# Moving and stationary operands of the rounded products placed 64 bytes apart, modulo 128

## The chip, the cores and the metric

One NeuronCore of a Trainium2 chip runs the whole program. The metric is device time in microseconds of one execution; the time before is the median of three runs.

## What is computed

The reference is one hybrid layer followed by two mixer layers, on 256 tokens of width 1024, all in float32. Cut to its products:

```python
h = rms_norm(x, norm1_gain)
p = h @ w_in                                  # 1024 x 6176: attention, recurrence, gates
...                                           # attention and a delta-rule recurrence
mixed = gates[..., :D] * y_att + gates[..., D:] * y_rwkv
x = x + mixed @ w_out
x = x + hierarchical_moe(rms_norm(x, norm2_gain), ...)   # 32 experts, top 2
for l in range(2):
    proj = rms_norm_2(x, ...) @ w_in[l]       # 1024 x 3072
    ...                                       # convolutions, two kinds of attention
    x = x + rms_norm_2(mix @ w_out[l], ...)
    f = conv_ffn(rms_norm_2(x, ...), w_up[l], w_conv[l], w_down[l])   # 1024 x 5632, 2816 x 1024
    x = x + rms_norm_2(f, ...)
```

## The kernel before, in words

The large dense products are computed in parts. A float32 operand is split into a rounded high part and the rounded rest, both in the type float32r, and a product is the sum of three: high with high, high with low, low with high. ScalarE writes the high part of a weight piece, VectorE subtracts and writes the low part, and TensorE then runs 8 matmuls (the 8 chunks of 128 of the 1024 inputs) for each part. A matmul has a stationary operand of 128 columns, which a weight load puts in place while the matmul before it runs, and a moving operand of 256 or 512 columns. The experts and most small products stay in float32 and aren't split.

The order is written out by hand for each engine, with semaphores. In the order of time: `front_part` (first projection, 17 pieces of 256 columns, matmuls at L595; three of the pieces, 6 to 8, have x stationary and the weight moving, the others the reverse); the recurrence, with float32 gate tiles in between (L225); `gate_in_parts` (L254), gate pieces 4 to 7, whose pairs of high and low weights lie in three buffers, `first` (pieces 4 and 7), `second` (5) and `third` (6); `mix_part` (L1708 and L1753), first the branch products with `branch_hi/lo`, then the out product with `mixed_hi/lo`, weights in `w_pair`; the experts (L2046 to L2103), whose weights stream into `expert_early`, `expert_ring` and `expert_top`; and `layers_part`, the two last layers, with `w_hi`, `w_lo`, `x_hi`, `x_lo`, `hid_hi` and `hid_lo`: entry products L2842, plain products L2868, value products L2880 with x stationary, and 512-column products L2904 with x or the hidden rows stationary.

SBUF places are given out in two ways. `Room(nc, at)` puts tensors at a fixed byte offset of every partition, one behind the other. `nc.sbuf_tensor` is a stack: it takes the next free place. Two offsets anchor the rooms: `m.room_at`, where the stack stands after the tensors that live long (56640, that is 64 modulo 128), and `m.ring_at`, the start of the experts' ring (81888, that is 96 modulo 128). Inside a tensor, all the slices that the rounded products use start at multiples of 128 bytes from its start, so the start of a tensor gives the place of all its operands modulo 128.

The transfers are issued by SyncE. The expert loads follow one another in ring slots; the first of them are issued between 200 and 270 us, behind waits on the gate, branch and out products.

Of the kernel before, what the change touches and what calls it, by code (L numbers as in the profile page):

```python
# [16 lines left out]
F32 = mybir.dt.float32  # L17
# [3 lines left out]
P = 128  # L21
# [147 lines left out]
KB = 1024  # L169
# [1443 lines left out]
def mix_part(nc, m, a, ctx):  # L1613
# [2 lines left out]
        return ctx.enter_context(nc.semaphore(n))  # L1616

    SPLITS = 2
    room = Room(nc, m.room_at + 8 * KB)
    mixed_hi, mixed_lo = room("mixed_hi", [P, KC, SEQ], F32R), room("mixed_lo", [P, KC, SEQ], F32R)  # L1620
    assert room.at <= m.ring_at
    room = Room(nc, m.ring_at + 64 * KB)
    branch_hi, branch_lo = room("branch_hi", [P, 6, SEQ], F32R), room("branch_lo", [P, 6, SEQ], F32R)
    part = room("gate_part", [P, 2, SEQ])
    room = Room(nc, m.ring_at + 80 * KB)
# [285 lines left out]
EARLY, SLOTS_R = 2, 10  # L1911
# [52 lines left out]
def moe_part(nc, m, a, out, recurrence):  # L1964
# [8 lines left out]
    with ExitStack() as ctx:  # L1973
# [3 lines left out]
        sb = m.room  # L1977
        rec_gpsimd, rec_sync, rec_scalar, rec_tensor, rec_vector = recurrence
        mix_sync, mix_tensor, mix_scalar, mix_vector = mix_part(nc, m, a, ctx)
        logits = sb("logits", [P, TT, NL])  # L1980
        group_max = sb("group_max", [P, TT, 1])
# [180 lines left out]

        assert m.room.at <= m.ring_at - 8 * KB
        layers_gpsimd, layers_sync, layers_tensor, layers_scalar, layers_vector = layers_part(nc, m, a, out, ctx)

        with nc.Block() as block:
# [461 lines left out]
def layers_part(nc, m, a, out, ctx):  # L2628
# [7 lines left out]
    def sb_r(n, s):  # L2636
        return ctx.enter_context(nc.sbuf_tensor(n, s, F32R))
    w_hi = Room(nc, m.room_at)("w_hi", [P, SPLIT, KC * 256], F32R)
    ctx.enter_context(nc.sbuf_tensor("below_layers", [P, (m.ring_at - m.room_at + EARLY * 16 * KB) // 4], F32))
    w_lo = sb_r("w_lo", [P, SPLIT, KC * 256])  # L2640
    x_hi = sb_r("x_hi", [P, KC, SEQ])
    x_lo = sb_r("x_lo", [P, KC, SEQ])
    vec = sb("vec2", [P, P])
# [767 lines left out]
def program(nc, a, out):  # L3411
    with ExitStack() as ctx:
        def sb(n, s):
            return ctx.enter_context(nc.sbuf_tensor(n, s, F32))
        m = Shared()
# [15 lines left out]
        with ExitStack() as one:  # L3431
# [4 lines left out]
            m.att_T = one.enter_context(nc.sbuf_tensor("att_T", [P, 2, SEQ], F32))  # L3436
            m.o_T = one.enter_context(nc.sbuf_tensor("o_T", [P, 4, SEQ], F32))
            m.room_at = nc.sbuf_base
            m.ring_at = (nc.sbuf_usable_end - 9 * 16 * KB) // 32 * 32
            ring = Room(nc, m.ring_at)  # L3440
            m.early = ring("expert_early", [P, EARLY, 2, 2 * D])
            m.first_rows = [one.enter_context(nc.semaphore(f"first_rows{f}")) for f in range(D_EXP // P)]
# [2 lines left out]
            m.landed = [one.enter_context(nc.semaphore(f"landed_{i}")) for i in range(SLOTS_R)]  # L3445
            m.gate_done, m.gate_taken = (one.enter_context(nc.semaphore(n)) for n in ("gate_done", "gate_taken"))
            m.gate_hi, m.gate_lo = (one.enter_context(nc.semaphore(n)) for n in ("gate_hi", "gate_lo"))
            top = Room(nc, m.ring_at + 8 * 16 * KB)
            m.x_hi, m.x_lo = (top(n, [P, KC, SEQ], F32R) for n in ("x1_hi", "x1_lo"))
            first, second, third = (Room(nc, at)(f"gate_pair{i}", [P, 2, KC, 256], F32R)  # L3450
                                    for i, at in enumerate((m.ring_at + 80 * KB, m.ring_at + 64 * KB, m.room_at + 8 * KB)))
            m.gate_pairs = (first, second, third, first)
            with ExitStack() as rec:
                m.w_up = rec.enter_context(nc.sbuf_tensor("w_up", [P, RW], F32))
# [59 lines left out]
```

How the kernel before makes its waits and increments, by code:

```python
def gate_landed(eng, m, g):  # L202
    eng.wait_ge(m.w_landed[gate_slot(g)], 16 * w_loads(gate_slot(g), g + 1, 0))
    return m.w_slots[gate_slot(g)]
# [10 lines left out]
def gate_tiles(pe, m, first, last):  # L216
    for n in range(first, last):
        half, k = divmod(n, KC)
        g, j = divmod(half, 2)
        if n % GATE_TILES == 0:
            gate_landed(pe, m, g)
        if k == 0 and half >= 2:
            pe.wait_ge(m.gate_taken, half - 1)
        mm = pe.matmul(m.ps[:, REC_BANKS + j, 0:SEQ], m.w_slots[gate_slot(g)][:, k, j * P:(j + 1) * P], m.hT[:, k, :],
                       start=(k == 0), stop=(k == KC - 1))
        if k == KC - 1:
            mm.then_inc(m.gate_done, 1)
# [8 lines left out]
def split_gate_low(dve, m, g):  # L237
    pair = m.gate_pairs[g - WHOLE]
    dve.wait_ge(m.gate_hi, g - WHOLE + 1)
    dve.tensor_tensor(pair[:, 1, :, :], m.w_slots[gate_slot(g)][:, :, :], pair[:, 0, :, :].bitcast(F32), ALU.subtract
                      ).then_inc(m.gate_lo, 1)
# [2 lines left out]
def gate_in_parts(pe, m, g, halves=(0, 1)):  # L245
    pair = m.gate_pairs[g - WHOLE]
    for j in halves:
        pe.wait_ge(m.gate_taken, 2 * g + j - 1)
        for part, (w, x) in enumerate(((0, m.x_hi), (0, m.x_lo), (1, m.x_hi))):
            if j == halves[0]:
                pe.wait_ge(m.gate_lo if w else m.gate_hi, g - WHOLE + 1)
# [6 lines left out]
def take_gates(act, m, first, last):  # L259
    for half in range(first, last):
        act.wait_ge(m.gate_done, half + 1)
        g, j = divmod(half, 2)
```

## Time and profile before

| | |
|---|---|
| median of 3 runs | 1359.61 us (1358.38 to 1361.61) |
| span of the profiled execution | 1355.0 us |
| TensorE busy | 1160.0 us, 86% of the span |
| VectorE busy | 737.7 us, 54% |
| ScalarE busy | 487.1 us, 36% |
| bytes read from HBM | 346.93 MB |
| 2868: 2880 matmuls of 256 columns | 134.2 + 134.1 + 132.3 us busy |

Busy times of TensorE are modelled and overlap from one matmul to the next, so a mean duration of 282 ns is not the time that a matmul adds to a run. The time per matmul is read from the starts: in the order of time each line gives the start of a group of alike matmuls and its count, and the difference to the next line's start, divided by the count, is the time of one.

### The profile page before, as it was taken

How to read it: one execution, taken by the hardware profiler on the slowest of the kernel's cores; microseconds unless marked ns; L12 is line 12 of the kernel's file. 1: busy time of each engine (PE TensorE's matmuls, PEld its weight loads, DVE VectorE, ACT ScalarE, POOL GpSimd, SP SyncE). 2: the span in 40 equal slices, each digit the busy share in tenths (PEclk: the TensorE clock that was granted, in tenths of full speed). 3: DMA queues.
4: the chain of work that ended last, by engine and by line, in shares of the span. 5: the costliest groups of instructions: out<-in, count | busy, mean ns of one | idle time of the engine just before them, and what ended most of it. 6: DMA issues, size and time to landing. Idle time of an engine off the chain costs nothing.

```text
span 1355.0 us, 22776 instructions
## 1 busy us (share of the span) xinstructions
PE 1160.0 (86%) x9669; PEld 919.5 (68%) x9669; DVE 737.7 (54%) x1120; ACT 487.1 (36%) x657; POOL 2.6 (0%) x11
## 2 busy tenths in 40 slices
PE   7999989997657366564739999999999999999998
PEld 6998778973213121221314998999998998999997
DVE  5487655852101010010104898877777899877776
ACT  4543435330000000000004546644446556644444
POOL 0000000000000000000000000000000000000000
PEclk9999999998878697788869999999999999999999
DMA  8842225999999999999999646566655436566650
GB/s 270 281 149 63 65 80 210 342 405 416 426 427 424 428 427 424 429 426 427 426 419 361 212 149 179 160 201 186 187 156 179 156 127 181 172 189 187 187 156 31
DMA packets 180986, 349.52 MB, mean 258 GB/s; under 512 B 8140, under 2 KB 154737, under 8 KB 167954
## 3 DMA queue, kind: packets, MB, share of 16 engines
q1 hardware_dynamic: 180394, 347.40, 70.6%
q8 instruction: 79, 1.29, 0.4%
q10 hardware_dynamic: 488, 0.62, 0.2%
q14 instruction: 25, 0.20, 0.0%
HBM read 346.93 MB, written 3.43 MB: 259 GB/s over the span
## 4 chain that ended last, share of the span: by engine, by line
PE 66%; DMA 17%; DVE 3%; issue 2%; SPq 1%; ACT 1%; DVEq 1%; ACTq 0%
PE ps L2868 25%; PE ps L2904 12%; DMA expert_ring<-in_w_expert_up 7%; PE ps L2058 6%; DMA expert_top<-in_w_expert_up 4%; PE ps L2089 4%; DMA expert_early<-in_w_expert_up 2%; DMA expert_ring<-in_w_expert_gate 2%; PE ps L225 2%; PE ps L2046 2%; PE ps L1708 2%; PE ps L2103 2%; PE ps L254 2%; PE ps L2880 2%; PE ps L2842 2%
## 5 line engine op out<-in xcount | busy, mean ns | idle before, releaser
L3216 DVE TENSOR_TENSOR w_lo<-expert_early,w_hi 128x2048 fp32r<-128x2048 f32 x80 | 182.8, 2291 | 25.7 <-ACT w_hi L3010 22.9
L2058 PE MATMUL ps<-expert_ring,w_slot 128*32 128x512 f32 x640 | 113.6, 712 | 96.7 <-DMA expert_ring<-in_w_expert_gate 40.9
L2131 DVE TENSOR_TENSOR hT<-ps,hT 128x512 f32<-128x512 f32 x8 | 8.5, 1068 | 340.9 <-PE ps L2058 340.9
L3010 ACT ACTIVATE w_hi<-expert_early 128x2048 fp32r<-128x2048 f32 x80 | 153.0, 1918 | 56.5 <-PE ps L2904 34.1
L2058 PEld LDWEIGHTS ps<-expert_ring,w_slot 128*32 128x32 f32 x640 | 30.3, 129 | 159.5 <-issue 159.5
L2868 PE MATMUL ps<-x_hi,w_hi 128*128 128x256 f32 x960 | 134.2, 282 | 0.0
L2868 PE MATMUL ps<-x_hi,w_lo 128*128 128x256 f32 x960 | 134.1, 282 | 0.0
L2868 PE MATMUL ps<-x_lo,w_hi 128*128 128x256 f32 x960 | 132.3, 280 | 0.0
L2868 PEld LDWEIGHTS ps<-x_hi,w_hi 128*128 128x128 f32 x960 | 122.9, 188 | 3.8 <-issue 1.6
L2868 PEld LDWEIGHTS ps<-x_hi,w_lo 128*128 128x128 f32 x960 | 123.0, 190 | 0.0
L2868 PEld LDWEIGHTS ps<-x_lo,w_hi 128*128 128x128 f32 x960 | 121.0, 188 | 0.0
L3392 DVE SCALAR_TENSOR_TENSOR ff<-ps,ff_taps,ff 128x254 f32<-128x254 f32 (+1 forms) x176 | 76.8, 478 | 46.5 <-ACT ff L3150 43.3
L3150 ACT ACTIVATE ff<-ps,ff_taps 128x256 f32<-128x256 f32 x88 | 36.9, 471 | 118.2 <-PE ps L2868 117.4
L2058 PE MATMUL ps<-expert_early,w_slot 128*32 128x512 f32 x192 | 51.5, 698 | 23.3 <-DMA expert_ring<-in_w_expert_gate 12.4
L2110 ACT ACTIVATE hT<-ps 128x512 f32<-128x512 f32 x8 | 4.8, 597 | 171.4 <-PE ps L2068 171.4
L2058 PE MATMUL ps<-const,w_slot 128*32 128x512 f32 x48 | 31.8, 827 | 33.1 <-DMA expert_early<-in_w_expert_up 20.5
L2108 ACT ACTIVATE hT<-ps 128x512 f32<-128x512 f32 x8 | 4.8, 597 | 146.4 <-PE ps L2058 146.4
L2089 PE MATMUL ps<-expert_ring,hT 128*32 128x512 f32 x288 | 47.7, 633 | 8.6 <-issue 6.8
L3227 DVE SCALAR_TENSOR_TENSOR att_T<-conf_pad,vec,att_T 128x256 f32<-128x256 f32 x120 | 52.8, 481 | 3.8
L2058 PE MATMUL ps<-expert_top,w_slot 128*32 128x512 f32 x96 | 52.4, 709 | 0.0
L2904 PE MATMUL ps<-w_hi,hid_lo 128*128 128x512 f32 x176 | 48.9, 396 | 0.0
L2904 PE MATMUL ps<-w_lo,hid_hi 128*128 128x512 f32 x176 | 48.8, 395 | 0.0
(531 smaller groups left out, 2095.5 us busy)
## 6 DMA issues: line engine op xcount, KB each, us to landing
expert_ring<-in_w_expert_gate SPq DMA_DIRECT2D x22, 2048.0 KB, 29.4
expert_ring<-in_w_expert_up SPq DMA_DIRECT2D x18, 2048.0 KB, 29.3
expert_early<-in_ffn_up SPq DMA_DIRECT2D x36, 1024.0 KB, 6.0
expert_ring<-in_w_expert_down SPq DMA_DIRECT2D x14, 2048.0 KB, 29.8
w_slot<-in_w_in SPq DMA_DIRECT2D x26, 1024.0 KB, 5.5
expert_early<-in_w_in SPq DMA_DIRECT2D x20, 1024.0 KB, 5.5
expert_early<-in_ffn_down SPq DMA_DIRECT2D x18, 1024.0 KB, 4.9
expert_early<-in_w_expert_gate SPq DMA_DIRECT2D x6, 2048.0 KB, 26.9
```

Of the source, the lines that this page charges most:

```text
L225: mm = pe.matmul(m.ps[:, REC_BANKS + j, 0:SEQ], m.w_slots[gate_slot(g)][:, k, j * P:(j + 1) * P], m.hT[:, k, :], start=(k == 0), stop=(k = ...
L254: mm = pe.matmul(m.ps[:, REC_BANKS + j, 0:SEQ], pair[:, w, k, j * P:(j + 1) * P], x[:, k, :], start=(part == 0 and k == 0), stop=(part == ...
L1708: mm = pe.matmul(out, w[:, pair_of(i), col:col + P], x[y][:, x0 + k, :], start=(p == 0 and k == 0), stop=(p == 2 and k == n - 1))
L2058: mm = pe.matmul(m.ps[rows_of(e), b, :], x_quad[:, k, rows_of(e)], w[e][:, k, :], start=(k == 0), stop=(k == KC - 1))
L2089: mm = pe.matmul(m.ps[rows_of(e), DOWN + j, :], hidden_T[:, f, rows_of(e)], w[e][:, f, j * 512:(j + 1) * 512], start=(f == 0), stop=(f == ...
L2868: mm = pe.matmul(m.ps[:, b, j * SEQ:(j + 1) * SEQ], w[:, s, at(k, j):at(k, j) + P], x[:, k, :], start=(part == 0 and k == 0), stop=(part = ...
L2904: mm = pe.matmul(m.ps[:, banks[2 * t + c], :], xs[:, chunk + k, t * P:(t + 1) * P], w[:, s, k * D + c * 512:k * D + (c + 1) * 512], start= ...
L3010: act.activation(w_hi[:, half_slot(l, i), :], raw_slot(m, i), ACT.Copy).then_inc(S["w_hi"], 1)
L3150: ins = act.activation(ff[:, n % 2, j, :], m.ps[:, b, at:at + SEQ], ACT.Copy, scale=ff_taps[:, 2, j * FF + n:j * FF + n + 1])
L3216: dve.tensor_tensor(w_lo[:, s, :], raw_slot(m, i), w_hi[:, s, :].bitcast(F32), ALU.subtract).then_inc(S["w_lo"], 1)
L3227: dve.scalar_tensor_tensor(conf[:, c, :], src, tap, conf[:, c, :], ALU.mult, ALU.add)
L3392: ins = dve.scalar_tensor_tensor(x, m.ps[:, b, at:at + SEQ - back], ff_taps[:, 2 - back, j * FF + n:j * FF + n + 1], x, ALU.mult, ALU.add)
```

## The change

Only places move. `m.ring_at` is rounded down to a multiple of 128 instead of 32 (81888 becomes 81792). The x operands of the first projection start 64 bytes further on in their room, so do the third gate pair and the branch operands. In the layers, a filler is 64 bytes longer and a small tensor of 64 bytes is put behind `w_lo`, which moves `w_lo` and everything behind it on the stack.

```diff
-    room = Room(nc, m.room_at + 8 * KB)
+    room = Room(nc, m.room_at + 8 * KB + 0)
     mixed_hi, mixed_lo = room("mixed_hi", [P, KC, SEQ], F32R), room("mixed_lo", [P, KC, SEQ], F32R)
     assert room.at <= m.ring_at
-    room = Room(nc, m.ring_at + 64 * KB)
+    room = Room(nc, m.ring_at + 64 * KB + 64)
     branch_hi, branch_lo = room("branch_hi", [P, 6, SEQ], F32R), room("branch_lo", [P, 6, SEQ], F32R)
...
     w_hi = Room(nc, m.room_at)("w_hi", [P, SPLIT, KC * 256], F32R)
-    ctx.enter_context(nc.sbuf_tensor("below_layers", [P, (m.ring_at - m.room_at + EARLY * 16 * KB) // 4], F32))
+    ctx.enter_context(nc.sbuf_tensor("below_layers", [P, (m.ring_at - m.room_at + EARLY * 16 * KB) // 4 + 16], F32))
     w_lo = sb_r("w_lo", [P, SPLIT, KC * 256])
+    sb("beside_w_lo", [P, 16])
     x_hi = sb_r("x_hi", [P, KC, SEQ])
...
-            m.ring_at = (nc.sbuf_usable_end - 9 * 16 * KB) // 32 * 32
+            m.ring_at = (nc.sbuf_usable_end - 9 * 16 * KB) // 128 * 128
...
-            top = Room(nc, m.ring_at + 8 * 16 * KB)
+            top = Room(nc, m.ring_at + 8 * 16 * KB + 64)
             m.x_hi, m.x_lo = (top(n, [P, KC, SEQ], F32R) for n in ("x1_hi", "x1_lo"))
             first, second, third = (Room(nc, at)(f"gate_pair{i}", [P, 2, KC, 256], F32R)
-                                    for i, at in enumerate((m.ring_at + 80 * KB, m.ring_at + 64 * KB, m.room_at + 8 * KB)))
+                                    for i, at in enumerate((m.ring_at + 80 * KB, m.ring_at + 64 * KB, m.room_at + 8 * KB + 64)))
```

The starts of the operands, modulo 128, before and after:

| product | stationary | moving | after |
|---|---|---|---|
| first projection, L595 | w 0 | x 96 | w 0, x 64 |
| first projection, pieces 6 to 8 | x 96 | w 0 | x 64, w 0 |
| gate, pairs first and second, L254 | pair 96 | x 96 | pair 0, x 64 |
| gate, pair third | pair 64 | x 96 | pair 0, x 64 |
| branch, L1708 | w_pair 96 | branch 96 | w_pair 0, branch 64 |
| out, L1708 and L1753 | w_pair 96 | mixed 64 | w_pair 0, mixed 64 |
| layers, L2842 and L2868, high weight part | w_hi 64 | x 96 | w_hi 64, x 0 |
| layers, the same, low weight part | w_lo 96 | x 96 | w_lo 64, x 0 |
| layers, L2880 and L2904, high weight part | x or hidden 96 | w_hi 64 | 0, w_hi 64 |
| layers, the same, low weight part | x or hidden 96 | w_lo 96 | 0, w_lo 64 |

## Rows read from the trace of the kernel before

**Rows 1.** Page, part 2: granted TensorE clock in tenths, 40 slices of 33.9 us.
```profile
PEclk9999999998878697788869999999999999999999
```
**Rows 2.** Windows: stretch, length, busy us (instructions) by engine, clock, DMA share, GB/s.
```profile
22.00:131.00 109.00, 107.40 (x902) 100.26 (x900) 74.31 (x97) 48.07 (x58) 0.00 (x0) 1.00 0.57 179
...
217.00:242.00 25.00, 25.00 (x197) 23.73 (x196) 18.42 (x18) 14.24 (x18) 0.00 (x0) 1.00 0.85 300
...
255.00:288.00 33.00, 32.82 (x276) 32.43 (x275) 22.22 (x27) 10.51 (x11) 0.00 (x0) 1.00 1.04 406
288.00:728.00 440.00, 269.08 (x1923) 107.45 (x1922) 56.93 (x134) 26.64 (x51) 0.00 (x0) 0.81 1.01 422
...
1163.00:1346.00 183.00, 183.00 (x1307) 171.76 (x1307) 137.95 (x194) 91.77 (x109) 0.00 (x0) 1.00 0.54 159
```
**Rows 3.** Waits of PE, first in 22 to 131 us, then in 740 to 1355 us.
```profile
PE ps L595 <- DVE w_lo L782: 0.2, 1, 0.2
...
PE ps L2842 <- DVE w_lo L3216: 0.5, 1, 0.5
```
**Rows 4.** Order of time, PE: start us, us; branch product, first and twenty-ninth matmul.
```profile
242.16 0.40 PE L1708 MATMUL ps<-branch_hi,w_pair 128*128 128x256 f32 x2
...
245.52 0.64 PE L1708 MATMUL ps<-branch_hi,w_pair 128*128 128x256 f32 x4
```
**Rows 5.** Order of time, PE: gate product, third pair, then first pair.
```profile
234.53 1.10 PE L254 MATMUL ps<-x_lo,gate_pair 128*128 128x256 f32 x8
235.47 2.06 PE L254 MATMUL ps<-x_hi,gate_pair 128*128 128x256 f32 x16
...
238.32 2.08 PE L254 MATMUL ps<-x_hi,gate_pair 128*128 128x256 f32 x16
240.24 1.12 PE L254 MATMUL ps<-x_lo,gate_pair 128*128 128x256 f32 x8
```
**Rows 6.** Order of time, PE: plain product of the layers, its three parts.
```profile
902.84 1.10 PE L2868 MATMUL ps<-x_hi,w_hi 128*128 128x256 f32 x8
...
904.72 1.12 PE L2868 MATMUL ps<-x_hi,w_lo 128*128 128x256 f32 x8
905.68 1.10 PE L2868 MATMUL ps<-x_hi,w_hi 128*128 128x256 f32 x8
```
**Rows 7.** Order of time, PE: first projection, weight stationary, then x stationary.
```profile
44.48 1.12 PE L595 MATMUL ps<-x_hi,w_hi 128*128 128x256 f32 x8
...
46.40 1.11 PE L595 MATMUL ps<-x_hi,w_lo 128*128 128x256 f32 x8
...
64.13 1.10 PE L595 MATMUL ps<-w_hi,x_hi 128*128 128x256 f32 x8
...
66.94 0.28 PE L595 MATMUL ps<-w_hi,x_hi 128*128 128x256 f32 x1
```
**Rows 8.** Chain of work that ended last: start us, us, what, count.
```profile
266.45 11.52 PE ps L1708 x96
...
484.67 3.57 PE ps L2046 x32
...
860.66 17.00 PE ps L2868 x144
```
**Rows 9.** Order of time, PE: 512-column product, 12 matmuls, then the next line's start.
```profile
914.14 1.09 PE L2904 MATMUL ps<-w_hi,hid_hi 128*128 128x512 f32 x4
...
916.93 0.75 PE L2868 MATMUL ps<-x_hi,w_hi 128*128 128x256 f32 x5
```
**Rows 10.** Groups by line and shape: busy us, mean ns | idle before; the split's low part.
```profile
L3216 DVE TENSOR_TENSOR w_lo<-expert_early,w_hi 128x2048 fp32r<-128x2048 f32 x80 | 182.8, 2291 | 25.7 <-ACT w_hi L3010 22.9 <-issue 1.1
...
L3216 DVE TENSOR_TENSOR w_lo<-w_slot,w_hi 128x2048 fp32r<-128x2048 f32 x18 | 41.3, 2293 | 7.4 <-ACT w_hi L3010 6.0 <-issue 0.9
```
**Rows 11.** DMA issues: count, KB each, median us from issue to landing.
```profile
expert_early<-in_ffn_up SPq DMA_DIRECT2D x36, 1024.0 KB, 6.0
...
w_slot<-in_ffn_up SPq DMA_DIRECT2D x8, 1024.0 KB, 6.1
```

## Prediction

> **What bounds the kernel now.** I read the granted clock first, then the busy time by stage, then who waits for whom, then the order of time inside the stages that TensorE bounds. The clock line [rows 1] stands at 9 tenths or more in the stages where the change acts; it dips only in the middle. The stage table [rows 2] splits the span in three. From 22 to 131 us (first projection) and from 217 to 242 us (gate product) TensorE is busy for nearly the whole stretch; from about 255 to 728 us the DMA engines are full (share 1.01 to 1.04, 406 to 422 GB/s) and TensorE has room; from 728 us to the end TensorE is busy all the time, in 1163 to 1346 us for 183.00 of 183.00 us. The waits [rows 3] agree: in the first projection the rounded operands hold TensorE up for 0.2 us, in the two last layers for 0.5 us. So the product runs as fast as TensorE takes its matmuls, and the quantity to look at is the time from the start of one matmul to the start of the next, called the spacing here. "Busy" in the profile overlaps and can't give it; starts in the order of time do.
>
> **The spacing by placement.** The rounded products differ in one thing that this change touches: where the stationary operand starts, modulo 128 bytes, against the moving one. "Below" and "above" say where the stationary one lies.
> - 0 apart. Branch product: 28 matmuls from 242.16 to 245.52 us, 120.0 ns each [rows 4]. Gate product, first and second pair: 16 in 238.32 to 240.24, 120.0 ns [rows 5]. Layers with the low weight part: 8 in 904.72 to 905.68, 120.0 ns [rows 6].
> - 32 apart, stationary below. Layers with the high weight part: 16 in 902.84 to 904.72, 117.5 ns [rows 6]. Gate product, third pair: 8 in 234.53 to 235.47, 117.5 ns [rows 5]; the same line of code, the same x operand, another pair buffer. First projection with x stationary: 24 in 64.13 to 66.94, 117.1 ns [rows 7].
> - 32 apart, stationary above. First projection with the weight stationary: 16 in 44.48 to 46.40, 120.0 ns [rows 7]; the out product: 96 in 11.52 us, 120.0 ns [rows 8].
> A whole run of 144 in the layers takes 17.00 us [rows 8], 118.1 ns; two parts at 117.5 and one at 120.0 would make 118.3, so the two levels carry the stage. The placement therefore shifts the spacing by 2.6 ns, and 117.4 (between 117.5 and 117.1) against 120.0 are the prices I use.
> The 512-column products run at 2.79 us for 12, 232.5 ns [rows 9]; they mix placements 0 and 32 apart, and I see no difference between their three parts.
> The Trainium skill, "TensorE: Matmul & The Clock Gate", Part 2, says that loading the next weights doesn't take read bandwidth from the running matmul, because the two operands have a read port each. By that rule no placement matters and the sum would be zero. Rows 5 disagree by 2.5 ns a matmul, so I don't take zero as my forecast, but it stays a rival.
>
> **What the change does, part by part.** No instruction, wait or transfer is added or removed. The three placements become one: 64 apart everywhere. Counts of 256-column matmuls on the path:
> - now at 120.0: first projection with the weight stationary 576, gate product 144, branch product 144, low weight part in the layers 960 + 64 + 64 (plain, entry and value products), value products with the high part 128. Together 2080, of which 864 lie before 250 us and 1216 in the layers.
> - now at 117.4: first projection with x stationary 144, third gate pair 48, high weight part in the layers 1920 + 128. Together 2240.
> - left out: the first piece of the first projection, 48 matmuls whose spacing waits for x.
> - not on the path: the out product, 192 matmuls at 266 to 288 us. The DMA engines are full there [rows 2], and what follows ends with a transfer. Its price is nothing; were the transfers not full there, it would be worth 192 x 2.6 ns = 0.5 us.
> With a spacing g after the change, the difference is 2080 x (g - 120.0) + 2240 x (g - 117.4) ns.
> The trace doesn't show 64 apart in a rounded product. Bounds: below, the nearest row with a weight load and a matmul that both last about as long as here is the gather product, 32 in 3.57 us, 111.6 ns [rows 8]: -17.5 - 13.0 = -30.5 us. Above, the worst placement seen, 120.0: +5.8 us. I take g = 117.4, the better of the two levels: three placements give 120.0 (0), 120.0 (32 above) and 117.4 (32 below), and a smooth wave through these three over 128 bytes gives 117.4 at 64 as well. That is 2080 x -2.6 ns = -5.4 us: -3.2 us in the layers and -2.2 us ahead of them.
> The -2.2 us pass through the stage that the transfers bound only if these start earlier. They do: the expert loads around 200 to 250 us are issued behind waits on the gate and branch products, whose inputs come from TensorE's order, and the full stretch then keeps its length.
> For the 512-column products (720) both placements seen cost the same, so I take 0; -1.8 us (230 ns, twice the 115 of the next part) and +1 us are the ends.
> What is late next: in 1163 to 1346 us VectorE is busy for 137.95 and ScalarE for 91.77 of 183.00 us [rows 2], so a matmul that is 2% faster finds its operands ready.
> Side effects. The whole ring moves from 96 to 0 modulo 128. The split on VectorE costs 2291 ns from a ring buffer (at 96) and 2293 from a weight slot (at 64) [rows 10]: the same. The loads of 1 MB land in 6.0 us in the ring and in 6.1 in the slot [rows 11]: the same. Both at nothing; if the full stretch of 440 us moved by 0.3% either way, 1.3 us.
>
> **Rivals.**
> 1. Placement at 64 removes more of the contention. The shape of the three points is thin evidence for a wave; the curve could dip at 64. With g = 115, about as far below 117.4 as this is below 120: -10.4 - 5.4 = -15.8, and -1.8 for the 512-column products, -17.6 us. Chance 0.18.
> 2. All of it goes: 111.6 and twice that for 512 columns (223.2): -30.5 - 6.7 = -37 us. Against it: the 512-column matmuls pay for a longer time than one weight load lasts, and all three placements pay at least 5.8 ns over 111.6, while placement moves 2.6. Chance 0.05. The same page of the Trainium skill, section "Back-to-back issue gap", gives N / 2.4 + 2.5, 109.2 ns for 256 columns; by it, used as an estimate, the sum would be about -41 us on these matmuls. No row of a rounded product comes near.
> 3. Slower: the contention repeats every 64 bytes, not every 128, so 64 apart is 0 apart again. Then g = 120.0: nothing is gained where it costs 120.0, and the high weight part of the layers, the largest group, loses 2240 x 2.6 ns = +5.8 us, with up to +1 for the rest. It decides from g = 118.7 on. For it: 0 apart is the worst placement, and nothing in the trace separates a period of 64 from one of 128 except that 32 above and 32 below differ. That difference speaks against a strict period of 64, not against a second dip and peak. Chance 0.20.
> 4. No change that can be measured, g between 118.0 and 119.3, or no effect of placement as such, or a buffer that doesn't end up where the text of the change says. Gains at 120.0 and losses at 117.4 cancel. Chance 0.17.
> My forecast has 0.40.
>
> **How the numbers follow.** The span is 1355.0 us, the median of the runs 1359.6; the 4.6 us around the span don't change. Forecast 1359.6 - 5.4 = 1354.2. The range reaches from rival 1 (1342) to rival 3 (1359.6 + 6.8 = 1366.4): I take 1343 to 1366, which leaves out rival 2 and the tails of 1 and 3. What a measurement of this kernel can tell from no change is about 0.2%, 2.7 us. Faster by more than that: 0.40 + 0.18 + 0.05 = 0.63, less 0.02 for the weak end of the forecast, 0.61. Within: 0.17 + 0.02 = 0.19. Slower: 0.20.
>
> **What would show it.** Right: in the order of time, 8 matmuls of any rounded 256-column product take 0.94 us from start to start, whichever part; a run of 144 in the layers takes 16.9 us, not 17.00; the first full transfer stretch begins 2 us earlier and is as long as before; the end comes 3 us earlier than that beyond. Wrong: 0.96 everywhere (rival 3), 0.92 or less (rival 1), 0.89 (rival 2). If the spacing falls and the end doesn't move, the step "TensorE bounds these stages" fails. If the full stretch changes its length, it is the transfers into the moved ring.

## The result and the profile after

The change takes 1346.82 us (1346.28 to 1348.65, 5 runs) against 1358.81 us for the kernel before in the same measurement: ratio 0.9917, 95% interval 0.9906 to 0.9927, 12.0 us less. A second measurement of the same kernel gave 1347.23 against 1358.21 us, ratio 0.9919 (0.9906 to 0.9933). The forecast was 5.4 us less. Work and counts are the same as before: 22776 instructions, 349.52 MB in the page's line on packets.

The clock stands at 9 tenths where it stood there before [rows 1], and the waits in the layers are of the same kind and size [rows 3]. What moved is seen in the order of time. In the chain of work that ended last (start us, us, what, count), the second layer part of the kernel after the change:

```profile
848.23 2.05 PE ps L2811 x16
850.28 5.52 PE ps L2843 x48
855.80 16.32 PE ps L2869 x144
872.12 5.57 PE ps L2905 x24
877.69 11.31 PE ps L2869 x96
889.00 5.57 PE ps L2905 x24
```

L2869 is L2868 of before, L2905 is L2904, and L2843, the entry product, is L2842. The 144 matmuls took 17.00 us before [rows 8] and take 16.32 now: 113.3 ns each, where the forecast had 117.4. The 96 behind them take 11.31 us: 117.8 ns each. So there is not one spacing for 64 apart but two, called the quick and the slow level below. The order of time of TensorE (start us, us, instruction, count) shows that each is steady over all three parts of the product. First the quick kind, then the slow one:

```profile
860.17 1.07 PE L2869 MATMUL ps<-x_hi,w_lo 128*128 128x256 f32 x8
861.08 1.07 PE L2869 MATMUL ps<-x_hi,w_hi 128*128 128x256 f32 x8
861.98 1.07 PE L2869 MATMUL ps<-x_lo,w_hi 128*128 128x256 f32 x8
862.89 1.07 PE L2869 MATMUL ps<-x_hi,w_lo 128*128 128x256 f32 x8
...
901.95 1.10 PE L2869 MATMUL ps<-x_hi,w_lo 128*128 128x256 f32 x8
902.89 1.11 PE L2869 MATMUL ps<-x_hi,w_hi 128*128 128x256 f32 x8
903.83 1.10 PE L2869 MATMUL ps<-x_lo,w_hi 128*128 128x256 f32 x8
904.78 1.10 PE L2869 MATMUL ps<-x_hi,w_lo 128*128 128x256 f32 x8
```

Starts 0.90 or 0.91 us apart for 8 matmuls are 113 ns; 0.94 or 0.95 are 118 ns. In [rows 6] the high weight part took 117.5 and the low part 120.0; the difference between the parts has gone, as it should when both weights lie 64 from x.

By stage, from the starts of the products: the layers' first rounded matmul starts at 737.17 instead of 739.77 us, 2.6 us earlier, and the span ends at 1346.0 instead of 1355.0. So 2.6 us were won ahead of the layers and 6.4 us in them (608.8 instead of 615.3 us). The 6.4 repeats in a second profile; the 2.6 belongs to this pair of executions. After the change the first rounded matmul of the first projection starts at 15.25 us, 1.8 us later than before (13.47). From there to the first expert matmul it takes 282.9 instead of 286.3 us, 3.4 less. The expert matmuls then stretch over 429.0 instead of 429.9 us, and over 429.1 to 431.8 in the other profiles of the block. The mean spacing over all plain, entry and value products of the layers, worked out from all starts in the trace with those over 150 ns left out, fell from 118.19 to 116.42 ns, and that of the 512-column products from 232.8 to 231.4. In the first projection the mean fell from 119.3 to 116.7, in gate and branch from 119.3 and 120.0 to 117.8.

### The profile page after: what moved, and what is told of

Same layout as the page of the kernel before. It is cut to its first block, busy times and chain, and to the rows that moved or that the text cites. A ratio compares the mean times of both kernels' runs of the same rounds, so it can differ in the third digit from the quotient of the medians.

```text
span 1346.0 us, 22776 instructions
## 1 busy us (share of the span) xinstructions
PE 1152.3 (86%) x9669; PEld 911.4 (68%) x9669; DVE 737.3 (55%) x1120; ACT 487.2 (36%) x657; POOL 2.6 (0%) x11
## 2 busy tenths in 40 slices
DMA packets 180986, 349.52 MB, mean 260 GB/s; under 512 B 8140, under 2 KB 154737, under 8 KB 167954
## 4 chain that ended last, share of the span: by engine, by line
PE 65%; DMA 17%; DVE 3%; issue 2%; SPq 1%; ACT 1%; DVEq 1%; ACTq 0%
PE ps L2869 25%; PE ps L2905 11%; DMA expert_ring<-in_w_expert_up 7%; PE ps L2058 6%; DMA expert_top<-in_w_expert_up 4%; PE ps L2089 4%; DMA expert_early<-in_w_expert_up 2%; DMA expert_ring<-in_w_expert_gate 2%; PE ps L225 2%; PE ps L2046 2%; PE ps L2103 2%; PE ps L254 2%; PE ps L1708 2%; PE ps L2881 2%; PE ps L2843 2%
## 5 line engine op out<-in xcount | busy, mean ns | idle before, releaser
L2058 PE MATMUL ps<-expert_ring,w_slot 128*32 128x512 f32 x640 | 116.3, 721 | 95.6 <-DMA expert_ring<-in_w_expert_gate 42.1
L3217 DVE TENSOR_TENSOR w_lo<-expert_early,w_hi 128x2048 fp32r<-128x2048 f32 x80 | 182.8, 2291 | 24.3 <-ACT w_hi L3011 21.5
L2869 PE MATMUL ps<-x_hi,w_hi 128*128 128x256 f32 x960 | 133.5, 282 | 0.0
L2869 PE MATMUL ps<-x_hi,w_lo 128*128 128x256 f32 x960 | 131.3, 278 | 0.0
L2869 PE MATMUL ps<-x_lo,w_hi 128*128 128x256 f32 x960 | 131.2, 279 | 0.0
L2869 PEld LDWEIGHTS ps<-x_hi,w_hi 128*128 128x128 f32 x960 | 122.1, 189 | 3.8 <-issue 1.6
L2869 PEld LDWEIGHTS ps<-x_lo,w_hi 128*128 128x128 f32 x960 | 120.6, 189 | 0.0
L2869 PEld LDWEIGHTS ps<-x_hi,w_lo 128*128 128x128 f32 x960 | 120.2, 187 | 0.0
L2905 PE MATMUL ps<-w_hi,hid_lo 128*128 128x512 f32 x176 | 48.8, 395 | 0.0
L2905 PE MATMUL ps<-w_hi,hid_hi 128*128 128x512 f32 x176 | 48.5, 393 | 0.0
```

The costliest lines, as they stand in the source:

```text
L2058: mm = pe.matmul(m.ps[rows_of(e), b, :], x_quad[:, k, rows_of(e)], w[e][:, k, :], start=(k == 0), stop=(k == KC - 1))
L2869: mm = pe.matmul(m.ps[:, b, j * SEQ:(j + 1) * SEQ], w[:, s, at(k, j):at(k, j) + P], x[:, k, :], start=(part == 0 and k == 0), stop=(part = ...
L2905: mm = pe.matmul(m.ps[:, banks[2 * t + c], :], xs[:, chunk + k, t * P:(t + 1) * P], w[:, s, k * D + c * 512:k * D + (c + 1) * 512], start= ...
L3217: dve.tensor_tensor(w_lo[:, s, :], raw_slot(m, i), w_hi[:, s, :].bitcast(F32), ALU.subtract).then_inc(S["w_lo"], 1)
```

## The experiments

The mean of a stage below is worked out as above; "quick" is the share of its 256-column spacings under 115 ns, which is the level of 113.3.

**The layers alone, and all the rest alone.** Both are the changed kernel with one side taken back.

```diff
--- the layers alone
-    ... EARLY * 16 * KB) // 4 + 16], F32))
+    ... EARLY * 16 * KB) // 4 + 24], F32))
...
-            m.ring_at = (nc.sbuf_usable_end - 9 * 16 * KB) // 128 * 128
+            m.ring_at = (nc.sbuf_usable_end - 9 * 16 * KB) // 32 * 32
...
-            top = Room(nc, m.ring_at + 8 * 16 * KB + 64)
+            top = Room(nc, m.ring_at + 8 * 16 * KB)
--- all the rest alone
-    ... EARLY * 16 * KB) // 4 + 16], F32))
+    ... EARLY * 16 * KB) // 4 + 24], F32))
-    sb("beside_w_lo", [P, 16])
```

(In the first, the third gate pair and the branch operands go back as well.)

> Only the operands of the two last layers are placed 64 bytes apart; the ring, the first projection, the gate and the branch products lie as in the kernel before. Theory (spacing of the rounded matmuls, stage by stage, adds up): the layers gained 6.4 us of span in the profile of the change, so 1358.8 - 6.4 = about 1352.4 us, ratio 0.995; the first transfer-bound stretch begins and ends as before (728 us). Rival (the gain is from the ring's new place and the transfers into it): no gain, 1358 to 1360.

Measured: 1354.95 against 1357.87 us, ratio 0.9974 (0.9964 to 0.9985), 2.9 us less.

> The reverse: everything ahead of the layers as in the change, the ring at 0 modulo 128 included, the layers' operands as before (w_hi 32 below x, w_lo at x). Theory: the end of the transfer-bound stretch comes 2.6 us earlier and the layers take as long as before: about 1356.2 us, ratio 0.998; with e1 it adds up to the whole. Rival (ring and transfers): nearly the whole gain of 12 us stands here.

Measured: 1353.37 us, ratio 0.9964 (0.9952 to 0.9976), 4.5 us less. Both sides gain, so the ring and its transfers aren't the cause of the whole. But the sum, 7.4 us, falls short of the 12.0, and the halves are the wrong way round. The traces say why in part. With the layers alone, the layers took 610.6 us (741.47 to 1352.1), 4.6 less than before, not 6.4; their quick share was 0.11, not the change's 0.32, although every operand lay at the same place modulo 128. With the rest alone, the layers took 615.2 us, as before, and the part ahead of them 4.7 us less than before; there the gate product ran with a quick share of 0.42 and the branch product with 0.99, at 113.4 ns, where the change's first profile had 117.8 for both. The same placement, then, gives different levels, and in the layers this is 1.8 of the 4.6 us that the sum lacks. The other 2.8 are about what three ratios with intervals of some 1.4 us either way leave open; no run settles them. The levels are what the next ones look into.

**32 below in the layers instead of 64.**

```diff
-    sb("beside_w_lo", [P, 16])
+    sb("beside_w_lo", [P, 8])
```

> The change, but x and the hidden rows of the layers stand at 96 and both weight parts at 64 modulo 128: in plain products the stationary operand lies 32 bytes below the moving one everywhere. Forecast's assumption (64 apart costs what 32 below costs): the same time as the change, 1346.8, and plain products at 117.4 ns. Theory after the result (64 apart has a second, quicker level of 113.3 ns that 32 below doesn't have): plain products at 117.4 without any run at 113.3, so the first 144 of each layer and each FFN take 16.9 us instead of 16.32, the 96 in the steady part 11.27 instead of 11.31: 2 to 4 us slower than the change, 1349 to 1351.

Measured: 1353.09 us, 4.8 less than the kernel before (0.9963, 0.9951 to 0.9975), and so 6 us more than the change has, where 2 to 4 more were expected. The chain has

```profile
856.88 16.98 PE ps L2869 x144
873.86 5.59 PE ps L2905 x24
879.45 11.33 PE ps L2869 x96
```

16.98 us for the 144 is 117.9 ns, a little over the 117.4 expected; the layers took 614.7 us, 0.6 less than before, with a quick share of 0.05. The forecast's assumption, 64 apart costs what 32 below costs, is refuted: it would have made this kernel as quick as the change. The price of 32 below itself doesn't hold here either. The low weight part of the plain and entry products went from 0 apart to 32 below, for which the prices give 1024 x -2.6 ns = -2.7 us, not 0.6. In the plain products its mean went from 119.5 to 117.4 ns, but those of the two parts with the high weights went from 117.5 and 117.3 to 118.2, although both their operands, `w_hi` and x, stand at the very addresses of the kernel before. The time of a part depends on where the operands of its neighbours in the stream lie, and a placement has no price of its own.

**The matmuls by themselves.** A kernel of its own, with the other engines idle while TensorE works (its loop, shortened: the calls leave out the bank of the result):

```python
for i in range(8):                            # the stationary operand 16 * i bytes above
    for _ in range(4): mm(kick[:, 0:P], kick[:, :])      # 512 columns
    run(i)                                    # 48 matmuls of 256 columns
    mm(kick[:, 0:P], kick[:, 0:64]);  run(i)
    mm(kick[:, 0:P], kick[:, 0:192]); run(i)
```

> Not the block at all: the computation is left out (zeros are stored) and only rounded matmuls with a weight load each run, in sets, with the stationary operand 0, 16, 32, ... 112 bytes above the moving one modulo 128. Each set of 48 is run three times, after 512 columns, after a matmul of 64 columns and after one of 192; then the set at 64 after matmuls of 16 to 240 columns; then 512-column sets. Theory (two levels, the level is set by the phase in which a run begins and kept): 0 gives 120.0 ns, 96 (that is 32 below) 117.4, 32 gives 120.0, and 64 gives 113.3 or 117.8 depending on what went before. Rival (the level depends on something else than the phase, such as the traffic of the other engines, which here are idle): 64 gives a single value after every prefix. If the contention repeated every 64 bytes, 64 would give 120.0, which the profile of the change already excludes.

The order of time of TensorE has, for the sets at 0, 32, 64 and 96 behind 512 columns, and at 64 behind 192 columns too:

```profile
32.60 5.92 PE L54 MATMUL ps<-x_moving,w_zero 128*128 128x256 f32 x48
38.35 0.20 PE L54 MATMUL ps<-kick 128*128 128x64 f32 x1
...
69.19 5.83 PE L54 MATMUL ps<-x_moving,w_thirtytwo 128*128 128x256 f32 x48
74.86 0.19 PE L54 MATMUL ps<-kick 128*128 128x64 f32 x1
...
105.52 5.82 PE L54 MATMUL ps<-x_moving,w_sixtyfour 128*128 128x256 f32 x48
111.17 0.20 PE L54 MATMUL ps<-kick 128*128 128x64 f32 x1
...
116.84 5.65 PE L54 MATMUL ps<-x_moving,w_sixtyfour 128*128 128x256 f32 x48
122.32 1.09 PE L54 MATMUL ps<-kick 128*128 128x512 f32 x4
...
141.48 5.80 PE L54 MATMUL ps<-x_moving,w_ninetysix 128*128 128x256 f32 x48
147.11 0.20 PE L54 MATMUL ps<-kick 128*128 128x64 f32 x1
```

From start to start, 48 take 5.75 us at 0 apart (119.8 ns), 5.67 at 32 above (118.1, where 120 was expected: a miss), 5.65 at 64 (117.7) and 5.63 at 96, which is 32 below (117.3). Behind 192 columns the set at 64 takes 5.48 us, of which the first takes 0.139; the other 47 take 113.6 ns. None of the seven other placements, behind any of the three prefixes, settles under 117. So of these sets only those at 64 apart reach the quick level. Each placement has a buffer of its own here and was tried at that one address. The sweep of prefixes at 64 apart, two of its fifteen sets (128 and 176 columns ahead):

```profile
207.42 3.86 PE L54 MATMUL ps<-x_moving,w_sixtyfour 128*128 128x256 f32 x32
211.11 0.70 PE L54 MATMUL ps<-kick 128*128 128x512 f32 x3
...
220.12 3.96 PE L54 MATMUL ps<-x_moving,w_sixtyfour 128*128 128x256 f32 x32
223.92 0.72 PE L54 MATMUL ps<-kick 128*128 128x512 f32 x3
```

3.69 us for 32 against 3.80, and the first of them took longer in the first case (0.172 against 0.149): the other 31 are at 113.5 and 117.8 ns. Behind 16, 64 to 160 and 192 to 224 columns the set settled at 113.3 after at most five matmuls; behind 32, 48, 176, 240 and 512 it stayed at 117.8 to its end. The level is thus set by how a run begins, and kept to the end of the set. It needs no other engine.

**The FFN's order by itself.** The same kind of kernel with 24 matmuls of 512 columns, then 48 of 256 at 64 apart, each order twice.

> Not the block: zeros are stored, and only the FFN's order of rounded matmuls runs, 24 of 512 columns (hidden rows stationary, 0, 32, 64 or 96 bytes above the weight), then 48 of 256 columns at 64 apart, each twice, without a matmul in between or with one of 16, 64, 128 or 192 columns. Theory (the level is set by the phase at the start): without one, at 64 apart in the 512-column set, 117.8 ns as in the profile of the change; with 64 or 128 columns in between 113.3; 512-column matmuls 0 apart take 227 to 230 ns, the others 231 to 234. Rival (the level needs the rest of the kernel): no pattern by what stands in between.

Without a matmul in between, the 48 ran at 117.8 ns where the hidden rows were 0 or 96 above the weights, and at 113.3 where they were 32 or 64 above, both times each. Behind one of 16, 128 or 192 columns 19 of 24 sets were quick; behind one of 64, 6 of 8. Three of the 20 orders (128 columns behind hidden rows at 64, 16 and 128 behind those at 96) were quick in one of their two turns and slow in the other, so what stands just ahead doesn't decide alone. The expectation for 64 apart (117.8) was wrong, the idea (what stands ahead decides) held: the place of the hidden rows doesn't touch the plain products, and yet their level changed with it. Which place gives which level doesn't carry over: in the block the plain products are slow behind hidden rows 64 apart and quick behind 0 apart, as the next runs show. The 512-column sets had means of 227.3, 233.1, 230.3 and 233.3 ns with the hidden rows at 0, 32, 64 and 96; for 64, 231 to 234 had been expected.

**In the kernel: another place for the hidden rows, and a short matmul ahead.** Both start from the change.

```diff
--- hidden rows 0 apart from the weights
+        ffn.enter_context(nc.sbuf_tensor("beside_silu", [P, 16], F32))
         hid_hi = ffn.enter_context(nc.sbuf_tensor("hid_hi", [P, 4, SEQ], F32R))
--- short matmul, in product(), where the piece before was a "down" piece
+                if kick:
+                    await_split(pe, l, "w_hi", i)
+                    pe.matmul(m.ps[:, b, 0:kick], w_hi[:, s, at(0, 0):at(0, 0) + P], x_hi[:, 0, 0:kick], start=True, stop=True)
```

> The change, but the hidden rows stand at 64 modulo 128, 0 apart from the weights, in the 528 products of 512 columns of the FFN. Theory: 232 ns become 227 to 230, 1 to 2.5 us less; the plain products behind them start in another phase and may take either level, at 113.3 another 8 us less: 1336 to 1346 us. Rival (64 apart is best for all shapes): 1 to 2 us more than the change.

> The change with one more matmul, of 128 columns, whose result is overwritten, ahead of each plain product of the FFN that follows a 512-column set; 20 in all. Theory (level set by the phase at the start): each costs 0.115 us, and the 96 matmuls behind it run at 113.3 instead of 117.8 ns, 0.43 us less: 20 x 0.31 = 6 us less than the change, about 1341 us, although there is more work. Rival (the level isn't set by the start): 2.3 us more, 1349 us.

> Both of the above. Theory: the gains add, 1338 to 1341 us. If the hidden rows' place already brings the plain products to 113.3, the short matmuls only cost: 2.3 us more than with the place alone.

Measured: 1339.99 us with the hidden rows moved (0.9866, 0.9850 to 0.9883), 1342.52 with the short matmul (0.9880, 0.9864 to 0.9897), 1341.29 with both (0.9874, 0.9857 to 0.9890). Moving the hidden rows, the chain has

```profile
856.16 16.32 PE ps L2870 x144
872.48 5.57 PE ps L2906 x24
878.04 10.89 PE ps L2870 x96
888.93 5.56 PE ps L2906 x24
```

(this is its second run, told below; the first has the same four durations but for 0.01), and with the short matmul, here at L2866, just ahead of the second of these stretches,

```profile
872.87 5.57 PE ps L2908 x24
878.50 10.95 PE ps L2872 x96
889.45 5.57 PE ps L2908 x24
```

In both, the 96 plain matmuls went from 11.31 to 10.9 us, 113.4 ns, and the quick share of the layers from 0.32 to 0.84 and 0.83. In the first the products whose operand was moved didn't change at all: 5.56 and 5.57 us for 24, where 5.45 to 5.52 had been expected. The layers took 601.2 instead of 608.8 us, and nearly all of that, 18 x 0.42 us, stands in the sets of 96, whose own operands didn't move. In the second, work was added and the kernel became 4.3 us quicker, 6 expected; its layers took 603.4 us. The expectation counted 20 short matmuls, but there are 18, nine in each layer. Both together take 1.3 us more than the place alone (2.3 expected): the cost of the short matmuls without a further gain.

**The same program twice, and beside it the better version.**

> The change as it is, run and profiled once more, beside the next two. If the level of a run is a matter of the program alone, the profile shows the same runs at 113.3 and the same at 117.8 as the first (first 144 of each layer quick, the FFN's 96 at 117.8, gate and branch at 117.8), and about 1346.8 us. If it is chance, some of them change their level between two executions, and the times scatter more than those of the kernel before.

> The hidden rows 0 apart once more, on the same chip as e7. Theory: again 7 us less than the change, all of it in the FFN's plain products (96 in 10.89 us), none in its 512-column products.

Measured: the change 1347.23 us, with the hidden rows moved 1341.17 (0.9874, 0.9859 to 0.9889), 6.1 us less on the same chip. In the layers the second profile of the change repeats the three durations of the first to 0.01 us (16.32, 5.57, 11.31; 608.9 us in all), and so does the quicker version's. Ahead of them it doesn't: the branch product, 48 matmuls, and the gate product before it are

```profile
224.96 14.89 PE ps L254 x128
239.85 5.45 PE ps L1708 x48
```

in the second profile and 5.67 us for the 48 in the first. So in the layers the level is a matter of the program; in the stage of the gates it also differs between executions of one program. Both answers that the expectation set against each other were right, each for its stage. Nine profiles have the changed part ahead of the layers without a further matmul in it; the branch product is quick in two of them, this one and the one with the rest alone, and slow in seven.

The order of time of TensorE shows where they part. Three lines of the gate product in the second profile of the change, then the same three in the first:

```profile
230.51 2.08 PE L254 MATMUL ps<-x_hi,gate_pair 128*128 128x256 f32 x16
232.44 1.07 PE L254 MATMUL ps<-x_lo,gate_pair 128*128 128x256 f32 x8
233.34 1.98 PE L254 MATMUL ps<-x_hi,gate_pair 128*128 128x256 f32 x16
...
231.48 2.15 PE L254 MATMUL ps<-x_hi,gate_pair 128*128 128x256 f32 x16
233.47 1.10 PE L254 MATMUL ps<-x_lo,gate_pair 128*128 128x256 f32 x8
234.41 2.05 PE L254 MATMUL ps<-x_hi,gate_pair 128*128 128x256 f32 x16
```

Up to the first of them both run at 117.8 ns. There two successive spacings are long, 182 and 223 ns in the one and 181 and 223 in the other. Behind this hold-up the one goes on at 113.3 ns and the other at 117.8. So a level lasts while the stream is unbroken, and nearly the same break can leave either.

**A short matmul ahead of the gate product.** The better version, with one more matmul of 128 columns.

> e8 with one more matmul of 128 columns ahead of the second run of the gate product (168 matmuls, behind which the 144 of the branch product follow). Theory: both at 113.3 instead of 117.8, 1.3 us earlier at the start of the out product, and as much less at the end, since the transfers start earlier by it. Rival: this run keeps 117.8 because each half waits on semaphores.

Measured: 1340.63 us, 0.5 less than e8's 1341.17, which the scatter doesn't separate. The 168 take 20.01 us and the 48 of the branch 5.67: still 117.8 ns. The expectation failed; 128 columns ahead is no recipe. The short matmul stands ahead of the part of the run before the hold-up, and that part stayed at 117.8 as well. What would make this run quick for certain wasn't found; a short matmul at the hold-up wasn't tried.

**The layers' operands 128 bytes further up.** Modulo 128 this moves nothing.

```diff
-    ... EARLY * 16 * KB) // 4 + 16], F32))
+    ... EARLY * 16 * KB) // 4 + 48], F32))
```

> The change with everything in the layers behind w_hi 128 bytes further up, which puts w_lo, x and the hidden rows where the first kernel, with the layers' part alone, had them; modulo 128 nothing moves. There the first 144 of each layer took 16.96 us in its profile, not 16.32, and the 512-column products 229.3 ns, not 231.9. If places modulo 128 are all that counts, and the rest is the phase in which the layers begin, this kernel's profile is like that of the change: 16.32 us, 231.9 ns, 1347 us. If places beyond 128 bytes count as well (w_hi stays where it is, so the distance from w_hi to x changes by 128), it is like the other: 16.96 us and 229.3 ns, +2.6 us for the four sets of 144 and -1.4 for the 512-column ones.

Measured: 1350.73 us, 0.9943 (0.9930 to 0.9957), 3.9 us more than the change. The chain has

```profile
857.33 16.96 PE ps L2869 x144
874.29 5.50 PE ps L2905 x24
879.79 11.31 PE ps L2869 x96
891.10 5.51 PE ps L2905 x24
```

The second reading holds in kind: all four sets of 144 are slow, and the 512-column products of the FFN take 229 ns (5.50 us for 24), as in the kernel with the layers' part alone, whose addresses these are. The size was missed: +2.6 and -1.4 us had been expected, and the layers took 611.5 us, 2.7 more than in the change. The entry products are 0.7 of it, with a mean of 117.8 ns instead of 114.3. The plain products' slow level is the same 117.8 as before. What the place modulo 128 fixes is which levels there are; which one a run takes hangs on things beyond it too. In the kernel with the layers alone one of the four sets of 144 took 16.32 us all the same, at

```profile
861.39 16.32 PE ps L2869 x144
```

so address alone doesn't decide either.

## Why the prediction was right, and where it wasn't

The direction, the range (1343 to 1366) and the bounding engine held. The time was 7.4 us under the forecast of 1354.2 and nearer to rival 1 (1342.0), for whose sake the range reached that far down, so that the range held is in part luck. These are the steps.

- "TensorE bounds these stages": right. The spacing fell and the end followed. Of 9.0 us of span, 6.4 were in the layers and 2.6 ahead of them; the forecast had 3.2 and 2.2. The transfer-bound stage handed on what it was given, within its scatter: its first matmul came 1.7 us earlier and its last 2.6, and with the rest alone 3.9 and 4.7.
- Spacing by placement, 120.0 and 117.4: right as rows of the kernel before, and the matmuls by themselves repeat 0 apart (119.8) and 32 below (117.3). The 32 above gave 118.1 there and 120.0 in [rows 7, 8], and with 32 below in all plain products the layers gained 0.6 us where these prices give 2.7. Even these placements have more than one pattern.
- g = 117.4 at 64 apart, by a smooth wave: the step that failed, the term that was mis-sized. It took one number where there are two, 117.8 and 113.3. With the layers' mean of 116.4 for g, its own formula gives 1216 x (116.4 - 120.0) + 2048 x (116.4 - 117.4) = -6.4 us for the layers, where 2048 of the 2240 lie, and the stage measured 6.4 less. The two agree by some luck: the measured means give 3264 x -1.77 ns = -5.8 us, and -1.0 for the 512-column products. The interpolation's value is within 0.4 ns of the slow level, so had there been only that, the layers' loss at the high weight part would have eaten most of the gain: 1216 x -2.2 + 2048 x 0.4 = -1.9 us.
- The 512-column products at 0, with -1.8 and +1 as ends: they gave 720 x -1.4 ns = -1.0 us, inside the ends.
- The high weight part of the layers, 117.4 before and after: wrong for the quick runs. The 144 that took 17.00 us took 16.32, and all three parts have 113.3 ns there.
- Side effects at nothing, right: the split on VectorE still costs 2291 ns a piece, the loads of 1 MB land in 6.1 and 6.2 us [rows 10, 11].
- 4.6 us around the span: wrong in kind. The five runs of the change have 1.8 us around their span (1347.79 with 1346.0, 1346.28 with 1344.5). So have later runs of the kernel before (1357.82 with 1356.0). Its profiled execution thus probably took 1356.8 us, 2.0 less than the median of 1358.8, and that of the change took 1.0 more than its median, which is why 9.0 us between the profiles are 12.0 between the medians. A difference of two spans of single executions carries that uncertainty.
- Rival 1 (more contention gone, g = 115) described a mean that no single run has: the kernel with the hidden rows moved has 114.1 in its layers, by having nearly all runs at one level and the rest at the other. Rival 2 (111.6) was not met; 113.3 is the lowest steady spacing in any run. Rival 3 (a period of 64) is excluded: 0 apart 119.8, 64 apart 117.7 and 113.6 in one kernel. Rival 4 is out by the interval. The rival of no effect of placement rested on the Trainium skill, "TensorE: Matmul & The Clock Gate", Part 2, by which a weight load takes no read bandwidth from the running matmul. That no placement matters, as the prediction read it, doesn't hold here: with nothing else running, and behind the same 192 columns, the matmuls after the first are 119.7 ns apart with the operands 0 apart (5.77 us for 48, of which the first takes 0.145) and 113.6 with them 64 apart. Whether it is read bandwidth that runs short, no run shows.

The best version found is the change with the hidden rows at 64 modulo 128, one more filler of 64 bytes: 1340.0 and 1341.2 us in two measurements, 0.9866 and 0.9874 of the kernel before. (With the short matmul ahead of the gate product it measured 1340.6, no different.)

## What to carry to other kernels

Read the distance from start to start of like matmuls, not their busy time, and compare it between products that differ in placement; where both operands are 4 bytes wide and weights are loaded for every matmul, try the two operands 64 bytes apart modulo 128. Then look whether each run is at one steady spacing, for there may be two: what stands ahead of a run, even a placement elsewhere or a short useless matmul, can decide, so a placement is to be timed in its kernel and its neighbours tried, and a stage profiled more than once before its level is believed. A price interpolated between three placements is a guess about a curve; here the fourth point had a second value that no curve through the others could show.

## What the runs showed of the hardware

- A stream of rounded 256-column matmuls with a weight load each settles in a repeating pattern, here at a granted clock of 1.00. 0 apart: 120.0 ns. 64 apart: 117.8 or 113.3 ns, whichever it falls into within some six matmuls. It stayed there for 144 matmuls in the layers (16.32 us), and changed in the gate product at two spacings of 182 and 223 ns.
- 512-column ones have levels of their own: 226.7 ns at 0 and 16 apart in the kernel of matmuls alone, 232 to 234 at the others; in the FFN of the block 232 or 229 at 64 apart, depending on places beyond 128 bytes.
- Adding 18 matmuls of 128 columns made the block 4.3 us quicker.
- What in the memory makes the two levels, and what beyond the place modulo 128 chooses between them (the phase at the start, a longer period of addresses, the arrival of a semaphore), stays open. So does why the time of one part of a product changes when only the operands of another part move (117.5 to 118.2 ns in the kernel with 32 below).
